# Chunk-band attention: one VectorE operation for bias, scale and row minimum over all 640 key columns

## The reference

```python
t = jnp.arange(CHUNK)[:, None]                       # CHUNK = 64
m = jnp.arange(A_BAND)[None, :]                      # A_BAND = 8 * 64 + 64
idx = jnp.clip(t + A_REACH - m, -128, 128) + 128
bias = jnp.take(rel_bias, idx, axis=1)
sc = jnp.einsum('blhd,bmhd->bhlm', qc, kb) * 64 ** -0.5 + bias
sc = jnp.where(valid, sc, -jnp.inf)
p = jax.nn.softmax(sc, axis=-1)
out = jnp.einsum('bhlm,bmhd->blhd', p, vb)
```

## Time and profile before

| what | value |
|---|---|
| time, median of 3 runs | 2213.66 us (2213.47 to 2219.09) |
| the profiled execution, its own time | 2211.12 us |
| its span | 2209.4 us |
| granted TensorE clock over the span, mean | 0.949 |
| attention's loop | 637 to 854 us: 217 us, 9.8% of the span |
| DVE busy in those 217 us | 166.60 us |
| PE busy | 160.19 us |
| ACT busy | 115.30 us |
| POOL busy | 0.00 us |
| one batch of 9 units, 640 keys each | 29.3 us |

### The profile page before, as it was taken

The page is one execution under the profiler, slowest core; times in us unless marked ns, Lnnn a source line. Parts: engine busy times, 40 slices in busy tenths (PEclk is TensorE's granted clock), DMA queues, the critical chain, the costliest instruction groups (busy, mean ns, idle before and its releaser), DMA issues. The chain is left out here.

```text
span 2209.4 us, 34183 instructions
## 1 busy us (share of the span) xinstructions
PE 1993.2 (90%) x13954; PEld 1788.8 (81%) x13954; DVE 821.3 (37%) x1578; ACT 666.7 (30%) x1277; POOL 585.9 (27%) x456
## 2 busy tenths in 40 slices
PE   4999999999977776677768999999999999999996
PEld 3999999999964554566658987988889999998884
DVE  3111676111147883244436418222222222222226
ACT  5101232000035554334435324522222222222222
POOL 8111112121100002412214424432222333333214
PEclk7999999999979997888878999999999999999998
DMA  4122224422162212021005423211111111111132
GB/s 123 56 90 88 83 91 153 156 91 90 68 209 97 77 39 77 2 88 40 26 19 158 130 96 116 85 39 48 39 39 39 46 50 39 48 39 48 39 115 86
DMA packets 159272, 169.19 MB, mean 77 GB/s; under 512 B 14187, under 2 KB 130043, under 8 KB 159150
## 3 DMA queue, kind: packets, MB, share of 16 engines
q1 hardware_dynamic: 152814, 141.52, 20.9%
q10 hardware_dynamic: 6336, 25.96, 2.9%
HBM read 126.84 MB, written 40.55 MB: 76 GB/s over the span
## 5 line engine op out<-in xcount | busy, mean ns | idle before, releaser
L2221 DVE TENSOR_TENSOR t_acc<-t_acc,t_B 128x512 f32<-128x512 f32 x270 | 184.9, 687 | 536.9 <-PE t_B L2319 536.8
L116 PE MATMUL i_ps<-x_hi,i_w_lo 128*128 128x384 f32 x1056 | 354.0, 335 | 0.0
L116 PE MATMUL i_ps<-x_lo,i_w_hi 128*128 128x384 f32 x1056 | 353.7, 335 | 0.0
L116 PE MATMUL i_ps<-x_hi,i_w_hi 128*128 128x384 f32 x1056 | 353.7, 335 | 0.0
L2299 PE MATMUL t_B<-t_merged_hi,t_wm_lo 128*128 128x384 f32 x768 | 256.9, 335 | 1.0 <-POOL t_wm_lo L1931 1.0
L2299 PE MATMUL t_B<-t_merged_lo,t_wm_hi 128*128 128x384 f32 x768 | 256.6, 334 | 0.0
L2299 PE MATMUL t_B<-t_merged_hi,t_wm_hi 128*128 128x384 f32 x768 | 256.6, 334 | 0.0
L106 POOL TENSOR_TENSOR i_w_lo<-i_w_raw,i_w_hi 128x1024 fp32r<-128x1024 f32 x44 | 104.8, 2383 | 444.4 <-ACT i_w_hi L101 444.4
L1931 POOL TENSOR_TENSOR t_wm_lo<-t_raw,t_wm_hi 128x1024 fp32r<-128x1024 f32 x48 | 116.3, 2422 | 319.6 <-ACT t_wm_hi L2003 319.6
L116 PEld LDWEIGHTS i_ps<-x_lo,i_w_hi 128*128 128x128 f32 x1056 | 199.1, 188 | 0.0
L116 PEld LDWEIGHTS i_ps<-x_hi,i_w_lo 128*128 128x128 f32 x1056 | 199.0, 188 | 0.0
(11 more groups left out here) (318 smaller groups left out, 3567.3 us busy)
## 6 DMA issues: line engine op xcount, KB each, us to landing
proj<-i_out ACTq DMA_DIRECT2D x44, 576.0 KB, 2.8
i_w_raw<-in_w_in SPq DMA_DIRECT2D x44, 512.0 KB, 3.9
t_raw<-in_w_up SPq DMA_DIRECT2D x32, 512.0 KB, 4.2
t_raw<-in_w_down SPq DMA_DIRECT2D x32, 512.0 KB, 3.6
t_gates<-proj SPq DMA_DIRECT2D x48, 192.0 KB, 2.7
a_k_cache<-in_cache_attn_k SPq DMA_DIRECT2D x8, 1024.0 KB, 5.9
a_v_cache<-in_cache_attn_v SPq DMA_DIRECT2D x8, 1024.0 KB, 5.2
d_c<-proj SPq DMA_DIRECT2D x3, 1536.0 KB, 7.3
```

The costliest lines, as they stand in the source:

```text
L116: last = pe.matmul(out, a[s][:, c, :], b[:, c, tokens], start=k == 0, stop=k == n - 1)
L2221: dve.tensor_tensor(a, a, B[(ND * j + d) % 4][:, :], ALU.add).then_inc(added, 1)
```

## The change

- `bias` grows from 256 to 640 columns a head, `bias_s` from 144 to 528. The far columns are filled by POOL, once: a copy of one column into 384 for all heads, a MEMSET of the unseen 64x64 corner into the bias itself, and, once SP's copies have landed, the same for `bias_s`. The semaphore `far_made` tells DVE.
- The bias is divided by the scale ahead (the two copies into `ext` become multiplications by 1/SC).
- `soft` of a prompt unit is one `tensor_tensor_reduce`: (scores + bias) * -SC to `s`, and its running minimum to `nmax`. That of a stream unit is two: the first 512 columns, whose minimum in `part` starts the second's over 128. `s_read` now comes with the end of that operation, minimum included.
- `s` holds negated scores, so the exponential has a scale of -1.
- `bias_own` is one row of 240 columns, read at a shifting offset, in place of 1152. Two of the five `s` tiles, `ext` and `stream_out` lie elsewhere in SBUF, in room that is free in this stage.
- The wait of `soft` on `p_made` (the exponential of five units ago) stands ahead of the operation and no longer ahead of the TENSOR_REDUCE.

```diff
@@ attention, sync @@
-                sp.dma_start(bias_s[h * TS:(h + 1) * TS, :], bias[0:TS, h, 0:P + TS]).then_inc(sb_in, 16)
+                sp.dma_start(bias_s[h * TS:(h + 1) * TS, FAR:], bias[0:TS, h, FAR:FAR + P + TS]).then_inc(sb_in, 16)
@@ attention, gpsimd @@
+            pool.wait_ge(pre_a, (NPRE + 1) // 2)
+            pool.wait_ge(pre_d, NPRE // 2)
+            step(pool.tensor_copy(bias[:, :, 0:FAR], bc(bias[:, :, FAR], 2, FAR)))
+            pool.memset(bias[64:P, :, 0:64], NEG).then_inc(far_made, 1)
+            pool.wait_ge(far_made, 1)
+            pool.wait_ge(sb_in, 16 * AH)
+            pool.tensor_copy(bias_s[:, 0:FAR], bc(bias_s[:, FAR], 1, FAR)).then_inc(far_made, 1)
@@ attention, scalar @@
-                    act.wait_ge(s_max, st + 1)
+                    act.wait_ge(s_read, st + 1)
...
-                    act.activation(x, x, ACT.Exp, bias=nmax[:, st % SR:st % SR + 1],
+                    act.activation(x, x, ACT.Exp, scale=-1.0, bias=nmax[:, st % SR:st % SR + 1],
@@ attention, vector: soft @@
+                    dve.wait_ge(p_made, u - SR + 1)
+                least = nmax[:, r:r + 1]
...
-                    if W > near:
-                        dve.tensor_scalar(x[:, 0:W - near], ps[:, 0:W - near], SC, bias[:, h, 0:1],
-                                          ALU.mult, ALU.add).then_inc(s_biased, 1)
-                        biased += 1
-                    dve.scalar_tensor_tensor(out=x[:, W - near:W], in0=ps[:, W - near:W], scalar=SC,
-                                             in1=bias[:, h, 2 * P - near:2 * P], op0=ALU.mult,
-                                             op1=ALU.add).then_inc(s_read, 1)
...
-                        dve.memset(x[64:P, 0:64], NEG).then_inc(s_biased, 1)
...
+                    if n > 2:
+                        dve.wait_ge(far_made, 1)
+                    dve.tensor_tensor_reduce(x[:, 0:W], ps[:, 0:W], bias[:, h, KEYS - W:], -SC, -NEG, ALU.add, ALU.min,
+                                             least).then_inc(s_read, 1)
...
+                        dve.wait_ge(far_made, 2)
+                    dve.tensor_tensor_reduce(x[:, 0:REACH], ps[:, 0:REACH], bias_s[:, 0:REACH], -SC, -NEG, ALU.add, ALU.min,
+                                             part[:, 0:1]).then_inc(s_part, 1)
+                    dve.wait_ge(s_part, b + 1)
...
+                    dve.tensor_tensor_reduce(x[:, REACH:KEYS], ps[:, REACH:KEYS], bias_own[:, P - TS - TS * b:2 * P - TS - TS * b], -SC, part[:, 0:1],
+                                             ALU.add, ALU.min, least).then_inc(s_read, 1)
...
-                dve.tensor_reduce(nmax[:, r:r + 1], x[:, 0:W], AX.X, ALU.max, negate=True).then_inc(s_max, 1)
```

More of the change, by code:

```diff
@@ L568, in stage_attention @@
                                            offset=env.ob_at + 4 * (NT - NPT // 2) * AW)
[L569 to L574 removed]
+        bias = sb("bias", [P, AH, KEYS])
+        FAR = KEYS - 2 * P
+        bias_s = sb("bias_s", [P, REACH + TS])
+        bias_own = sb("bias_own", [P, 2 * P - TS])
+        rb = sb("rb", [AH, 2 * NR + 1])
+        spare = env.ob_at + 4 * (NT - NPT // 2) * AW + 4 * CONV
+        ext = nc.alloc_sbuf_tensor_at("a_ext", [AH, 3 * P], F32, offset=spare)
+        so = nc.alloc_sbuf_tensor_at("a_stream_out", [P, P], F32, offset=spare + 12 * P)
+        assert spare + 16 * P <= env.tail_at
         kc = [sb(f"k_cache{i}", [P, 4, AW]) for i in range(2)]
@@ L580, in stage_attention @@
         qd = [sb(f"q_diag{i}", [P, 4, 2 * TS]) for i in range(2)]
-        s = [sb(f"s{i}", [P, KEYS]) for i in range(SR)]
+        late = env.c_at + 4 * CC * 256
+        s = [sb(f"s{i}", [P, KEYS]) if i < 3 else nc.alloc_sbuf_tensor_at(
+            f"a_s{i}", [P, KEYS], F32, offset=late + 4 * KEYS * (i - 3)) for i in range(SR)]
+        assert late + 8 * KEYS <= env.c_at + 16 * T
         nmax, rsum, rinv = sb("nmax", [P, SR]), sb("rsum", [P, SR]), sb("rinv", [P, SR])
+        part = sb("part", [P, 1])
         pt = [sb(f"p_t{i}", [P, KEYS]) for i in range(2)]
-        so = sb("stream_out", [P, P])
         S = [c.enter_context(nc.psum_tensor(f"a_S{i}", [P, 1024], F32)) for i in range(2)]
@@ L706, in pre_read @@
             else:
[L707 removed]
+                dst, src = bias[:, 2 * t:2 * t + 2, FAR:], bank.rearrange("p (h m) -> p h m", h=2)
             copy(dst, src).then_inc(sem, 1)
@@ L782, in soft @@
[L782 to L792 removed]
+                    W = n * P
@@ L798, in soft @@
-                    dve.tensor_scalar(x[:, 0:3 * P], ps[:, 0:3 * P], SC, bias_s[:, 0:1],
-                                      ALU.mult, ALU.add).then_inc(s_biased, 1)
-                    dve.scalar_tensor_tensor(out=x[:, 3 * P:4 * P], in0=ps[:, 3 * P:4 * P], scalar=SC,
-                                             in1=bias_s[:, 0:P], op0=ALU.mult, op1=ALU.add).then_inc(s_biased, 1)
+                        dve.tensor_copy(bias_own[:, P - TS:P], bias_s[:, REACH:]).then_inc(bias_made, 1)
+                        dve.wait_ge(far_made, 2)
```

39 lines of the change are left out of this document (8 added, 31 removed).

## The result

The kernel before takes 2213.7 us in the median (2213.5 to 2219.1 in the four runs beside the changed kernel), the changed kernel **2189.5 us** (2188.9 to 2193.6, four runs). The profiled execution took 2188.92 us (2211.12 before), with a span of 2187.2.

What follows compares the result with a forecast made beforehand. DVE was taken to set the attention loop's pace, with PE waiting for it. The terms 10.2 + 3.3 + 3.1 + 0.4 - 1.2 - 0.3 = 15.5 us, off 2213.7, gave 2198.2 us; range 2190 to 2209.

Steps and rivals of the forecast that it cites:

- The operation: DVE's fused operation in `soft`: 0.82 us over 640 columns, 0.17 for the read-out, a wide unit 1.98 us against 2.96.
- Half rate: Rival: the fused operation runs at half rate, 1.49 us over 640 columns, giving 2206.7 us; chance 0.09.
- slower: Rival: the fused operation costs more than the passes it replaces, some 14 us lost at 2.2 us, 2227; chance 0.06.
- (a): PE's value matmuls waiting for DVE's copy out of O: the wait goes, gain 10.2 us.
- (b): PE waiting for the stream's copy and the query copies in DVE's queue: gain 3.3 us.
- (c): PE's scores waiting for DVE's reading of the prompt's S: gain 3.1 us, with 0.9 of 4.0 kept.
- (d): PE's scores waiting for DVE's reading of the stream's S: stays and grows, loss 0.15 a batch, 1.2 us in eight.
- (e): The loop's tail, behind the last scores: the reduction leaves, the stream's pieces add 0.15 to 0.3, gain 0.4 us.
- (f): POOL's fills: the large copy is covered, but the `bias_s` copy may delay the first stream, loss 0.3 us.
- the prediction's ceiling of 3.3: A wide batch: not more than 3.3 of 29.3 us can be gained, however much DVE is relieved.
- Another wait takes its place: Rival: `soft` shortens but another wait, ACT's above all, loses 11 of the 15.5 us, 2209.5 us; chance 0.07.
- More than the sum: Rival: PE's second half-clock dip and kept waits may go too, 22 us saved, 2191.5 us; chance 0.08.

Runs made afterwards that it cites:

- e2: Changed kernel with the fused operation split into one bias pass (SCALAR_TENSOR_TENSOR) that signals s_read, then a TENSOR_REDUCE for the maximum, in all units: 2199.2 us, ratio 0.9925.
- b1: The kernel before, unchanged, profiled a second time: 2219.5 us (one execution).
- b2: The kernel before, unchanged, profiled a third time: 2211.6 us (one execution).
- e10: Changed kernel plus a useless TENSOR_REDUCE over the bias behind the fused operation and its signal, in every prompt unit: 2197.8 us, ratio 0.994.
- e11: Changed kernel with a useless TENSOR_REDUCE behind the signal in every prompt unit, the same kernel profiled once more: 2202.0 us (one execution).
- e7: Kernel before with PE turning probabilities ahead of the score pair at each batch's fifth step, and DVE's copy out of O ahead of `soft`: 2204.5 us, ratio 0.995.
- e0: The changed kernel, unchanged, run and profiled again beside the kernel before: 2188.6 us, ratio 0.989.
- e5: Changed kernel plus a useless TENSOR_REDUCE over the bias behind the signal, only in the second and third batches' prompt units: 2192.9 us, ratio 0.991.
- e6: Changed kernel with PE turning probabilities ahead of the score pair at each batch's fifth step, and DVE's copy out of O ahead of `soft`: 2186.3 us, ratio 0.987.
- e8: Changed kernel with POOL assembling the stream's bias row, so a stream is one fused operation over 640 columns: 2190.3 us, ratio 0.9895.
- e9: Changed kernel with both the stream in one fused operation and the probabilities turned ahead of the score pair at the fifth step: 2182.0 us, ratio 0.986.
- e12: The changed kernel, unchanged, profiled a third time: 2189.3 us (one execution).
- e4: Changed kernel with the fused operation of each prompt unit done twice, the second one signalling; streams as they are: 2203.7 us, ratio 0.996.
- e1: Changed kernel's layout, POOL fills and 640-column bias, but `soft` with the old operations and signals of the kernel before: 2212.1 us, ratio 0.999.
- e3: Changed kernel plus a useless TENSOR_REDUCE behind each fused operation, which now gives the signal s_read: 2214.1 us, ratio 0.9995.

## Why the prediction was wrong, and what of it was right

The direction, the mechanism and the division by waits were right; the size was 9 us short. Two steps failed: the waits were priced by the rows' idle times (15.5 us, and they were worth 18.1), and the half-clock stretch of one profiled execution was taken for the kernel's own (4.7 us). By its own steps:

**The operation.** Predicted 0.82 us, measured 0.82; the read-out was put at 0.17 us of DVE's time, and costs none. The unit is 1.61 us, not 1.98. It changes no term, since DVE has time to spare in either case. Half rate (1.49 us) and slower are excluded by that duration, and by e2: with and without the minimum it is the same. DVE is busy for 15.9 us of a wide batch, where I had 18. The rule of the Trainium skill on two-source operations (Vector Engine (DVE) Microarchitecture Reference, section 7) would not bite with a source in PSUM, and the trace agrees with that: 819 ns for 640 columns.

**(a)**, the copy out of O: predicted 10.2 us, and the rows give 13.3 - 2.36 = 10.9 before and 2.1 - 1.6 = 0.5 after: 10.4. **(b)**, the stream's copy and the queries: 3.3 and 3.3, and the 0.5 us that its turn in the tail waits for the stream's copy, before and after, was in no term. **(c)**, the prompt's reading of S: 3.1, measured 4.0 - 1.2 = 2.8; all that is left lies in the first batch. **(d)**, the stream's reading: -1.2, measured 4.1 - 4.7 = -0.6; the two read-outs cost 0.12 us at the first and nothing at the second, not 0.17 each. **(e)**, the tail: 0.4; it is 12.3 us long and not 13.0, so 0.8. **(f)**, POOL's fill: -0.3; its large copy takes 2.74 us and not 4.0, and the last one ends at 651.0, before the first stream's scores are there, and costs nothing. What I did not have is 0.8 us more at the transposes that wait for DVE's scaling (0.4 to 1.2), for which see the last section. By the rows 25.1 - 9.2 = 15.9 us of waits are gone, where the terms said 15.5. The loop counted from 637 us, as in the prediction, is 196 us and not 201 to 202, and the wide batch 26.05 and not 26.5.

**Where the terms were read short.** The idle time that a matmul's row gives is less than what the wait costs. PE's timeline of a pair and the values behind it, the kernel before and the changed kernel:

```profile
815.47 1.31 PE L937 MATMUL a_O<-a_p_t,a_v_tok 128*64 128x128 f32 x20 [0.58 <-DVE oa_ob L828]
```

```profile
769.92 1.35 PE L886 MATMUL a_S<-k,q 64*128 64x512 f32 x8 [0.52 <-DVE a_nmax L807]
771.20 1.31 PE L934 MATMUL a_O<-a_p_t,a_v_tok 128*64 128x128 f32 x20
```

Before, the values start 815.47 - 813.54 = 1.93 us behind the pair, with a wait of 0.58 between them; in the changed kernel, with no wait, 771.20 - 769.92 = 1.28. The wait was worth 0.65. The matmul ends are modelled. Over a whole wide batch the rows say 2.9 us less for six waits fewer, and the starts 3.28: each wait is short by 0.06 to 0.07 us. That is also why the batch gained 3.28 us, as much as the prediction's ceiling of 3.3, with half a microsecond of the stream's wait still there. A check of the whole loop: without any stretch at half clock it would be before, from the batches that have none, 22.57 (b1) + 22.57 + 25.09 + 28.81 + 29.09 + 29.34 + 29.09 (b2) + 13.02 (tail of the first profile) = 199.6 us; the changed kernel's is 181.5: **18.1 us** are the waits, where I had 15.5. The rows inside the loop give 23.4 - 7.2 = 16.2 us for 29 waits fewer (40 before, 11 after), and 29 times 0.06 to 0.07 are the other 1.9.

**The clock.** This is the step that failed most. I took the second stretch at half clock for a part of the kernel, gave its absence 1.9 us as a rival of 0.08, and took the difference between the profiled execution and the median, 2.5 us, for a constant. It is neither: over three executions the loop before is 204.3 us on average, 4.7 above its 199.6, and the changed kernel's is never above 181.5. The offset of 2.5 us was the before's clock in its median runs (the profiled one had 0.949, all of them 0.9458 on average), and does not belong to the changed kernel, whose profiled execution lies 0.6 us under its median. 18.1 + 4.7 = 22.8 us in the loop; the remaining 1.4 lie in the other stages, where the same kernel differs by 3 to 7 us from one execution to the next, so that nothing can be read from it.

**Does the change itself hold the clock up?** The table is in favour: the seven executions with 11.3 us of waits or less have 0 or 1 us at half clock, the four with 14 to 18 have 6 to 10, the six with more than 22 have 8 to 26. e10 and e11, which differ from the changed kernel in one useless operation, go with it. It holds within each of the four comparisons that were run side by side (e7 has 13 us where e0, e5 and e6 have none; b1 and b2 23 and 14 where e8 and e9 have 0 and 1; e10 and e11 6 where e12 has 1; e2 and e4 7 and 10 where e1 and e3 have 24 and 26). Against a simple rule is that the stretches lie now here and now there, and that e7 with its 22.7 us is free of them up to 832. So it is an association over 17 executions, with one intervention that gave the smaller part of what it should; that PE's waits for DVE bring the stretches is supported and not shown. What a further wait would need to be, and where, to bring one about stays open.

**The rivals.** "Another wait takes its place" is excluded: PE's waits for ACT's copies are 10.9 + 10.7 us at the two kinds of turns before and after. "More than the sum" is what happened, but not as it was put: the stretch at half clock is missing in three profiles, while what I kept in (a) and (c) stayed (0.5 us for the 0.7 kept, and 1.2 for the 0.9). Its own numbers do not add up either: 15.5 + 1.9 + 0.7 + 0.9 are 19.0 us, not the 22 from which it gave 2191.5. That 2191.5 lies near the measured time is luck. Of the signs of being wrong that the prediction named (a slow operation, ACT's waits growing, a clock that falls) none came; a clock that stays up was not among them.

## What to carry to other kernels

When an engine is relieved that another waits for, add up the waits that end at its signals, and measure what each is worth from start to start in two places of the timeline, once with the wait and once without it, rather than by the idle time in the row. Look at where an added operation stands to the signal: in prompt units alone 0.75 us behind it cost this kernel 8 to 9 us (e10) and ahead of it 14 (e4), in all units 10 (e2) and 25 (e3), a part of each by the clock. And before a stretch at a lower clock enters a sum, profile the same kernel two or three times: the comparison of mean clocks over many runs tells more than the stretch in one of them.
